# Expert weight loads of a two-layer mixture-of-experts trunk, cut into DMAs of 1024 columns

## What is computed

```python
def moe_ffn(h, w_router, b_router, w_gate, w_up, w_down):
    aff = jax.nn.sigmoid(jnp.einsum('ntd,de->nte', h, w_router))
    ...
    combine = jnp.sum(jax.nn.one_hot(top_idx, N_EXPERTS) * top_w[..., None], axis=-2)
    hg = jnp.einsum('ntd,edf->ntef', h, w_gate)
    hu = jnp.einsum('ntd,edf->ntef', h, w_up)
    act = jax.nn.silu(hg) * hu * combine[..., None]
    return jnp.einsum('ntef,efd->ntd', act, w_down)
```

## Time and profile before

| | |
|---|---|
| median of three runs | 1544.51 us (1544.26 to 1546.76) |
| the profiled execution | 1547.95 us, span 1546.3 us |
| TensorE busy | 1432.9 us, 93% of the span |
| ScalarE, VectorE, GpSimd busy | 40%, 52%, 11% |
| granted TensorE clock, mean | 0.963 |
| DMA packets | 55861, 239.75 MB |
| queue q1 (SyncE), share of 16 engines' span | 39.0% |
| queue q0 (GpSimd), share of 16 engines' span | 6.0% |
| experts of layer 1, first weight load after the preloaded ones to last down | 573.7 to about 744 us |
| experts of layer 2, the same | 1335.9 to about 1509 us |

### The profile page before, as it was taken

The page is one execution under the profiler, slowest core; times in us unless marked ns, Lnnn a source line. Parts: engine busy times, 40 slices in busy tenths (PEclk is TensorE's granted clock), DMA queues, the critical chain, the costliest instruction groups (busy, mean ns, idle before and its releaser), DMA issues. The chain is left out here.

```text
span 1546.3 us, 23017 instructions
## 1 busy us (share of the span) xinstructions
PE 1432.9 (93%) x9168; PEld 1166.6 (75%) x9168; DVE 800.9 (52%) x1351; ACT 612.4 (40%) x1156; POOL 171.3 (11%) x152
## 2 busy tenths in 40 slices
PE   7999899999999959989799999999999998799895
PEld 6897665999997846656478966669999976566563
DVE  3224767433333766656842257673333347766565
ACT  3322578322222226656323326772222212465550
POOL 3012000000000112222112210000000001122230
PEclk9999899999999969999899999999999998799997
DMA  8334400322223759997423143021222256599953
GB/s 269 87 124 159 143 2 2 110 80 85 89 69 109 286 187 334 341 317 268 143 109 120 56 169 134 2 76 56 89 75 90 65 202 244 203 342 341 326 173 125
DMA packets 55861, 239.75 MB, mean 155 GB/s; under 512 B 11718, under 2 KB 19796, under 8 KB 45964
## 3 DMA queue, kind: packets, MB, share of 16 engines
q1 hardware_dynamic: 44716, 216.08, 39.0%
q0 software_dynamic: 11040, 22.21, 6.0%
HBM read 224.55 MB, written 34.49 MB: 168 GB/s over the span
## 5 line engine op out<-in xcount | busy, mean ns | idle before, releaser
L1435 PE MATMUL ps<-xT_high,w_high 128*128 128x288 f32 x704 | 208.0, 295 | 0.0
L1436 PE MATMUL ps<-xT_low,w_high 128*128 128x288 f32 x704 | 207.2, 294 | 0.0
L1437 PE MATMUL ps<-xT_high,w_ring_low 128*128 128x288 f32 x704 | 206.3, 293 | 0.0
L1533 ACT ACTIVATE tanh_gate<-ps 128x576 f32<-128x576 f32 x48 | 31.3, 652 | 295.8 <-PE ps L1437 295.8
L1437 PEld LDWEIGHTS ps<-xT_high,w_ring_low 128*128 128x128 f32 x704 | 132.6, 188 | 0.0
L1436 PEld LDWEIGHTS ps<-xT_low,w_high 128*128 128x128 f32 x704 | 132.5, 188 | 0.0
L1435 PEld LDWEIGHTS ps<-xT_high,w_high 128*128 128x128 f32 x704 | 132.1, 188 | 0.0
L1843 PE MATMUL ps<-down,hidT 128*128 128x512 f32 x256 | 118.0, 604 | 4.2 <-ACT hidT L1894 2.4
L1585 DVE SCALAR_TENSOR_TENSOR branch_part<-tanh_gate,ps 128x576 f32<-128x576 f32 x32 | 24.1, 754 | 176.5 <-ACT tanh_gate L1533 176.5
L1327 POOL TENSOR_TENSOR ln_rs<-ln_mv,const 128x1 f32<-128x1 f32 (+1 forms) x20 | 17.5, 873 | 868.7 <-DVE ln_mv L1322 868.7
L557 PE MATMUL ps<-z_w_high_part,oT_low 128*128 128x454 f32 x260 | 97.3, 374 | 8.7 <-DVE z_w_ring_low L1041 8.7
(11 more groups left out here) (368 smaller groups left out, 3314.5 us busy)
## 6 DMA issues: line engine op xcount, KB each, us to landing
gate_up<-in_we SPq DMA_DIRECT2D x34, 2048.0 KB, 12.2
down<-in_we SPq DMA_DIRECT2D x32, 1024.0 KB, 10.2
w_ring<-in_wm SPq DMA_DIRECT2D x28, 640.0 KB, 4.1
z_w_ring<-in_wtm SPq DMA_DIRECT2D x30, 454.0 KB, 4.1
w_ring<-in_wm SPq DMA_DIRECT2D x16, 768.0 KB, 4.5
w<-in_w SPq DMA_DIRECT2D x2, 2048.0 KB, 8.8
sel_pages<-in_sel_pages SPq DMA_DIRECT2D x32, 128.0 KB, 2.0
win_rows<-in_win_rows SPq DMA_DIRECT2D x2, 2048.0 KB, 8.1
```

Source lines behind the costliest of these rows:

```text
L1435: pe.matmul(out, w[0], x[0], start=first, stop=False)
L1436: pe.matmul(out, w[0], x[1], start=False, stop=False)
L1437: return pe.matmul(out, w[1], x[0], start=False, stop=last)
```

## The change

Each load of gate and up becomes four DMAs of 1024 columns, each load of down two. They are issued one after the other and add to the same semaphore; whoever waits for the load now waits for 64 or 32 counts in place of 16. A packet is 4096 bytes. The order of the work on every engine, and all waits besides these counts, stay as they are.

```diff
+GU_COLS = [slice(n * 1024, (n + 1) * 1024) for n in range(4)]
+DOWN_COLS = [slice(n * 1024, (n + 1) * 1024) for n in range(2)]
+GU_LOADED, DOWN_LOADED = 16 * len(GU_COLS), 16 * len(DOWN_COLS)
...
             for n in range(RING_E):
-                sp.dma_start(k.gu[:, n, :], io["we"][l, n, :, 0:4096]).then_inc(k.gu_in[n], 16)
+                for cols in GU_COLS:
+                    sp.dma_start(k.gu[:, n, cols], io["we"][l, n, :, cols]).then_inc(k.gu_in[n], 16)
...
-                    act.wait_ge(k.gu_in[0], 16)
+                    act.wait_ge(k.gu_in[0], GU_LOADED)
...
                 def load_gu(ch, e):
-                    sp.dma_start(gu[:, ch.raw, :], io["we"][l, e, :, 0:4096]).then_inc(gu_in[ch.raw], 16)
+                    for cols in GU_COLS:
+                        sp.dma_start(gu[:, ch.raw, cols], io["we"][l, e, :, cols]).then_inc(gu_in[ch.raw], 16)
 
                 def load_dw(ch, e):
-                    sp.dma_start(dw[:, ch.dslot, :], io["we"][l, e, :, 4096:6144]).then_inc(dw_in[ch.dslot], 16)
+                    for cols in DOWN_COLS:
+                        sp.dma_start(dw[:, ch.dslot, cols], io["we"][l, e, :, 4096 + cols.start:4096 + cols.stop]
+                                     ).then_inc(dw_in[ch.dslot], 16)
...
-                    pe.wait_ge(dw_in[ch.dslot], ch.d_nth * 16)
+                    pe.wait_ge(dw_in[ch.dslot], ch.d_nth * DOWN_LOADED)
...
-                    act.wait_ge(gu_in[ch.raw], ch.raw_nth * 16)
+                    act.wait_ge(gu_in[ch.raw], ch.raw_nth * GU_LOADED)
```

## The result

The changed kernel takes 1552.7 us (median of 20 runs), the one before 1546.8 in the same session; the ratio is **1.0041, 95% interval 1.0028 to 1.0054**: slower, by 6 us. The forecast was +4.7 us, on 1544.5. Loads are now lines 1745 and 1749, gather 1955, scatter 1959, the casts of gate and up 1890, the output copies 1910 and 1911, the transposes of gathered rows 1817, down 1852.

A forecast was written before the change was run, and what follows sets the result against it. The prediction took the loaded half of the DMA engines as the bound of the experts' stages: +2.4 us in layer 1, +1.7 in layer 2, +0.6 in the tails, +4.7 on 1544.5, so 1549.2 us, range 1534 to 1559.

The forecast's parts named there:

- Scatters and late rows wait no more: Experts' stages: output copies stop waiting for scatters and TensorE for gathered rows, as scatters land in 7 to 8 us.
- The saving of 2.4 us: Scatter and gather queue: each lands some 2.4 us sooner, waiting behind 8 packets for 1.3 us in place of 3.7.
- The cast becomes the place: ScalarE's cast of gate and up waits for its loads once their 2.6 us of slack is used up.
- The loaded half is the bound: Main case, chance 0.47: half the DMA engines carry the first 64 slots and need 11.3 to 12.0 us a chunk.
- The packets: Weight loads: smaller packets cost +0.23 us a gate/up load and +0.10 a down load, +4.1 us a layer.
- 6.4 of work less 3.0 of slack: Layer 1, cast of chunk 15: packets +4.1 and scatter 11 +2.3 us, engines empty from 716.0; 3.4 us later.
- the tail: End of each layer: ScalarE waits longer for the unused load of chunk 16, +0.3 us each.
- Packets near 73000: Sign that the prediction is right: the whole kernel's DMA packets go from 55861 by 17152 more.
- Layer 2: Second layer's experts' stage: the cast moves +2.7 us, less 0.96 of ScalarE idle time, +1.7; its tail +0.3.
- The waits simply go: Rival, chance 0.20: all 16 chunks run at TensorE's 10.13 us, -22.2 us, 1522.3 us; half of it, 1533.
- The loads suffer more: Rival, chance 0.13: four DMAs to a load mean four completions and turns, +10 us a layer, 1560 or more.
- Nothing is served differently: Rival, chance 0.20: turns aren't by packets, scatters land as today, slack hides most packet cost; 1544.5 up to 1547.

The follow-up runs named there:

- e9: The kernel before, weights' packets untouched (16384 and 8192 bytes), with each chunk's rows spread over the slots in steps of four: 0.9879 of the kernel before.
- e12: The changed kernel (4096-byte packets) with each chunk's rows spread over the slots in steps of four: 0.9857 of the kernel before.
- e8: The kernel before with only gate/up loads cut into 4096-byte packets, down loads left whole at 8192: 0.9974 of the kernel before.
- e11: The changed kernel measured once more, nothing else altered: 1.0041 of the kernel before.
- e5: The change with pieces of 512 columns, eight DMAs to a gate/up load and four to a down load, packets of 2048 bytes: 1.0043 of the kernel before.
- e6: The change with each gate/up load in two DMAs of every other 1024-column piece instead of four, packets still 4096 bytes: 1.0068 of the kernel before.
- e10: The kernel before with all weights' packets at 8192 bytes and rows spread over the slots in steps of four: 0.9857 of the kernel before.
- e1: As many DMAs as the change, but loads cut by partitions (32 or 64 rows), packets staying 16384 and 8192 bytes: 1.098 of the kernel before, 1701 us.

## Why the prediction was right, and where it was not

- *Scatters and late rows wait no more*: right. No output copy waits for a scatter in either layer, and TensorE only once for a gathered row (0.2 us, layer 2). GpSimd still waits 17.6 us for scatters in layer 1 and 48.3 in layer 2, without an output copy waiting behind it. A scatter was to land in 7 to 8 us and takes 9.5. The saving of 2.4 us was right (2.3); the start wasn't, since I took 9 to 10 us from GpSimd's idle time, where issue to landing is 11.9. The gather's gain was put at the same 2.4 us; it was 6 to 7, as it also stands behind the scatter.
- *The cast becomes the place, from chunk 7, at 11.3 to 12 us a chunk*: right, from 627.60 us on and 11.8 us. The load of chunk 8, issued at 620.54, is cast 18.8 us later (I expected landings up to 18). The 11.3 has no working in the prediction: the weights' 7.4 us and 16 rows at 161 ns, as the stores run alone, are 10.0, less than 10.13. Only with the 287 ns of a row in the full stage does a loaded engine need 12.0, and that price held: with even engines a row takes about as long (e9, 604 to 684 us: queue q0 21.9% of 16 engines for 1080 rows, 260 ns each).
- *The loaded half is the bound*: right, and the point on which all hangs. I had inferred it from a share of 0.49, which was thin: that window lies shortly before the engines ran empty at 1474.6. The spreads show it by moving rows alone, and the loads' semaphores show a pause of 1.05 to 2.63 us between eight engines and the other eight. That the other half has nothing to do isn't shown: the mean share of 0.98 counts it as busy too.
- *The packets*: +4.1 us a layer was too little in layer 1. From the first load to the cast of chunk 15 it was 718.99 - 573.74 = 145.25 us and is 721.90 - 571.86 = 150.04: +4.8, where 6.4 of work less 3.0 of slack gave +3.4. The 0.96 us of idle ScalarE time was taken as forecast (from this cast to the next output copy 9.17 us before, 8.21 now). So +3.8 at that copy where I had +2.4, and the tail cost 0.8, not 0.3. The weights' engine time per MB rose by 6.3% in 604 to 684 us, where 0.33 us on 7.4 is 4.5%: 91.2 us of weights on the loaded engines x 6.3% = 5.7 in place of 4.1, about what is missing at the cast. But the same packets on even engines are dearer by 1.5% only, 40.0 us per MB in e9 and 40.6 in e12 (fence below the list). What in the full stage makes up the rest is open; a packet's time there includes waits for other packets, and by e8 layer 1 loses only once the down loads are halved too.
- *Packets near 73000*: 75159. The 17152 more of weights are there, and the 134 further DMAs bring 16 packets under 512 bytes each, 2144 (13862 against 11718 on the two pages), which I had left out.
- *Layer 2*: +0.5 us in place of +2.0. Its cast comes 1488.78 - 1339.97 = 148.8 us after the first load, +1.4 against a before of 147.4, so the sum came out at 5.2 against 4.7 partly because two errors cancel. In e11 the same stage is +1.6: one profile doesn't settle a microsecond.
- *The waits simply go* (a chance of 0.20): wrong here, and yet the mechanism is real. Its condition was that a loaded engine needs less than 10.13 us for a chunk, and where the rows are spread that holds: 1523 to 1527 us against its 1522.
- *The loads suffer more*, by completions and turns of their own: out. e5 has twice the DMAs of the change and takes the same time, e6 has fewer and isn't faster.
- *Nothing is served differently*: out, by the landing times. That turns go by packets fits every landing time from 16384 down to 4096 bytes: scatters 11.9, 10.9 and 9.5 us, gathers 15.0, 12.4 and 7.8. These kernels also differ in how full the engines are; under the spread in steps of four, where that is small, the order is the same (e9, e10, e12): scatters 9.7, 9.1 and 8.3 at most, gathers 10.5, 8.7 and 7.2.

The queue of the weights, 604 to 684 us, in e9 and in e12 (packets, MB, share of 16 engines):

```profile
q1 hardware_dynamic: 2301, 25.14, 78.6%
```
```profile
q1 hardware_dynamic: 6879, 25.05, 79.5%
```

So the change bought shorter scatters for longer loads on engines that had room for neither. What the prediction missed was outside the change: of the 23.6 us over TensorE's own time, 22.3 went by moving rows to other slots (stages of e9).

## What to carry to other kernels

When a mean DMA share near 1 bounds a stage, ask which engines carry the work: an indirect DMA that fills only the first slots of a tile can load some engines more than the others, and spreading the rows in steps of four slots took some 20 us off the kernel before (0.988) without a byte less. Packet size on one queue bears on how long a small transfer on another waits; halving 16384 helped at almost no price, quartering it and halving the down loads cost more than it gave as long as the engines were unevenly full. Price a packet in the mix it will run in, not alone. Cut loads by columns: cut by 32 partitions they ran at half the rate here.

## What the runs showed of the hardware that I had not expected

- DMAs onto 32 partitions ran at 221 GB/s with a share of 1.06, against 422 onto 128, with twelve issued one after the other (e1).
- In the kernel before, a load's 16 additions to its semaphore come in two groups of eight, 1.05 to 2.63 us apart; with the rows in steps of four (e9) that pause is at most 0.22 us.
- Packets of 2048 bytes gave 330 GB/s alone, 410 at 4096, 422 at 16384, but the kernels with 2048 and 4096 took the same time (1.0043 and 1.0041).
- In the window of 664 to 684 us the engines moved 322 GB/s at a share of 0.98 before and 372 at 0.97 in e9, which differs from it only in the slots of the rows: the share doesn't tell how much is left.
